# One DiT layer in float32 on one core: mod rounds written out, square sums on VectorE, three full low-rank tiles, 512-column matmuls in merge, output and down

## What is computed

```
mod   = silu(c) @ w_mod + b_mod                    # 6 x 2048 values, also for the context
h     = rmsnorm(x) * (1 + sc1) + sh1               # and the same for the context tokens
p     = h @ w_in                                   # k, r, v, 4 x 96 low-rank, 256 gate columns, u, v, gates
y     = rwkv7(dwconv1d(p...))                      # both directions, over context and latents
yg    = gelu(u) * (w_spatial @ LN(gelu(v)) + b)    # chunk MLP
m     = sigmoid(ga) * (y @ w_proj_a) + sigmoid(gb) * (yg @ w_proj_b)
x     = x + gt1 * rmsnorm(m @ w_out)
h2    = rmsnorm(x) * (1 + sc2) + sh2
x     = x + gt2 * rmsnorm((silu(a) * b) @ w_down)  # a, b = dwconv2d(h2 @ w_up)
```

## Time and profile before

| | us |
|---|---|
| median of 3 runs | 2997.85 (2994.82 to 2999.31) |
| the profiled execution | 2995.07 |
| its span, first to last instruction | 2993.1 |
| PE busy in it | 2841.4 (95%) |
| DVE busy | 1839.5 (61%) |
| ACT busy | 1002.5 (33%) |
| stages by the timeline: mod to 115.5, lora to 192.3, pairs to about 1656, gv and gu to 1741.5, merge to 2071.3, out to 2174, up to 2711, down to 2975 | |

### The profile page before, as it was taken

One profiled execution on the slowest core, in us unless ns is written; L12 is line 12 of the kernel. 1 busy time (PEld: TensorE's weight loads), 2 busy tenths in 40 slices (PEclk: granted clock), 3 DMA queues, 4 the chain that ended last, 5 costly groups with the idle time before them and its releaser, 6 DMA issues.

```text
span 2993.1 us, 70020 instructions
## 1 busy us (share of the span) xinstructions
PE 2841.4 (95%) x27808; PEld 2207.5 (74%) x27808; DVE 1839.5 (61%) x3324; ACT 1002.5 (33%) x1715; POOL 579.6 (19%) x708
## 2 busy tenths in 40 slices
PE   5899999999999999999989999999989999999997
PEld 1246665566656566666556699999979999999997
DVE  1115666677666767666675544444378888885434
ACT  1123322333322333332231433333354444443333
POOL 0003222333122233222231110000013333330000
PEclk9799999999999999999999999999989999999998
DMA  8621332222332222233214545554525555554553
GB/s 323 268 77 63 107 107 93 70 74 89 103 107 93 82 75 86 93 106 107 79 53 148 204 148 182 186 182 170 198 99 183 182 182 182 182 182 156 182 174 134
DMA packets 75291, 412.28 MB, mean 138 GB/s; under 512 B 9200, under 2 KB 11888, under 8 KB 42736
## 3 DMA queue, kind: packets, MB, share of 16 engines
q1 hardware_dynamic: 74352, 407.51, 39.5%
q0 software_dynamic: 768, 2.10, 0.2%
HBM read 405.38 MB, written 4.19 MB: 137 GB/s over the span
## 4 chain that ended last, share of the span: by engine, by line
PE 84%; DVE 8%; issue 3%; DMA 3%; ACT 1%; SPq 0%; DVEq 0%; ACTq 0%; PEldq 0%
PE PB L671 18%; PE Q L919 6%; PE Q L920 6%; PE Q L924 6%; PE PB L919 4%; PE PB L920 4%; PE PB L924 4%; PE CH L924 3%; PE CH L920 3%; PE CH L919 3%; DMA ring<-w_mod_dram 3%; PE Q L808 3%; PE PB L656 2%; PE Q L794 2%; PE Q L815 2%
## 5 line engine op out<-in xcount | busy, mean ns | idle before, releaser
L671 PE MATMUL PB<-hT,ring 128*128 128x512 f32 (+1 forms) x1536 | 673.5, 552 | 6.4 <-PEq L660 5.4
L1615 DVE TENSOR_TENSOR w_lo_r<-ring,w_hi_r 128x1536 fp32r<-128x1536 f32 (+3 forms) x178 | 386.9, 2174 | 269.8 <-ACT w_hi_r L1217 269.8
L1217 ACT ACTIVATE w_hi_r<-ring 128x2048 fp32r<-128x2048 f32 (+2 forms) x178 | 325.8, 1831 | 453.7 <-PE Q L924 211.3
L671 PEld LDWEIGHTS PB<-hT,ring 128*128 128x128 f32 x1536 | 256.8, 189 | 120.9 <-issue 70.7
L920 PE MATMUL PB<-hT_r,w_hi_r 128*128 128x256 f32 x832 | 204.6, 285 | 0.0
L1475 DVE SCALAR_TENSOR_TENSOR arena<-ring,csilp,arena 128x512 f32<-128x512 f32 x240 | 193.5, 806 | 5.2 <-DMA ring<-w_mod_dram 1.0
L1775 DVE TENSOR_TENSOR w_lo_r<-ring,w_hi_r 128x1408 fp32r<-128x1408 f32 x62 | 101.2, 1633 | 147.9 <-ACT w_hi_r L1331 147.9
L1876 POOL TENSOR_TENSOR w_lo_r<-ring,w_hi_r 128x512 fp32r<-128x512 f32 x88 | 118.4, 1346 | 361.4 <-ACT w_hi_r L1217 361.4
L919 PE MATMUL PB<-hT_r,w_hi_r 128*128 128x256 f32 x704 | 175.7, 289 | 4.7 <-DVE hT_r L1702 4.7
L919 PE MATMUL Q<-ff_hi_r,w_hi_r 128*128 128x256 f32 x704 | 175.6, 288 | 1.8 <-ACT w_hi_r L1331 1.8
L920 PE MATMUL Q<-ff_lo_r,w_hi_r 128*128 128x256 f32 x704 | 172.9, 284 | 0.0
(11 more groups left out here) (266 smaller groups left out, 6096.5 us busy)
## 6 DMA issues: line engine op xcount, KB each, us to landing
ring<-w_up_dram SPq DMA_DIRECT2D x88, 1024.0 KB, 4.8
ring<-w_mod_dram SPq DMA_DIRECT2D x128, 512.0 KB, 3.7
ring<-w_rkv_dram SPq DMA_DIRECT2D x48, 1024.0 KB, 5.8
ring<-w_down_dram SPq DMA_DIRECT2D x64, 704.0 KB, 4.0
ring<-w_mod_dram SPq DMA_DIRECT2D x32, 1024.0 KB, 7.8
ring<-w_ga_dram SPq DMA_DIRECT2D x16, 1024.0 KB, 4.8
ring<-w_gb_dram SPq DMA_DIRECT2D x16, 1024.0 KB, 4.8
ring<-w_pa_dram SPq DMA_DIRECT2D x16, 1024.0 KB, 4.8
```

The costliest lines, as they stand in the source:

```text
L671: last = mm(PB[slot % 2][:, 0:cols], tile(n, kt), hT[:, kt, 0:cols], start=(kt == 0), stop=(kt == KT - 1))
L1217: f(w_hi_r[:, r % 2, 0:n], ring[:, r, 0:n], ACT.Copy).then_inc(hi_rdy, 1)
L1615: tt(w_lo_r[:, r, 0:n], ring[:, r, 0:n], as_f32(w_hi_r[:, r % 2, 0:n]), ALU.subtract).then_inc(lo_rdy, 1)
```

## The change

- **Constants and x.** Six constants (those that mod needs) are loaded first; the other eight follow behind the first lora weight tile, on a semaphore of their own (`consts2_ld`), for which ACT, DVE, PE (before the first `item`) and POOL wait. x comes in four quarters behind the four regions of mod round 0.
- **Mod rounds.** The loop is written out. The rounds alternate between banks Q[0] and Q[1]; the sums of round i-1 stand between the second and third region of round i, the last ones inside the first lora tile (before kt 4).
- **Square sums.** ACT squares by quarters; DVE adds the 16 tiles down to one; PE runs one 512-column matmul against ones in round 2. `hT` is scaled by quarters in rounds 3 to 6, and a quarter of h is made (DVE and ACT) as soon as its column gains are there, in rounds 4 to 7.
- **Low-rank columns.** The 384 columns are packed in 3 tiles of 128; five DMAs inside SBUF move the rows to the four places of 96 that the heads read. `lora` loads go from (2, 2, 1, 1) to (2, 1, 1, 1): the last gate tile is in region 0. The heads' first projection waits for bank 0 only; sigmoid and moves are waited for before the first `item`.
- **512 columns.** In merge, out and down the two 256-column matmuls with w_hi become one with 512 columns (hi and lo side by side), w_lo goes on into one half, and DVE adds the two halves of the bank (`halves`, a tensor_reduce). ACT takes sigmoid and square from SBUF after that. For the gates the high half of h is copied next to the low one by ACT in gu round 1. gu and up keep 256 columns.
- **Tables.** Three `preload_act_table_set` for the set with Ln and Exp are added: before the gv statistics, before out, and before down (one at the start was there).

```diff
-            for t, name in ((ident, "ident"), (ones, "ones"), ... 13 constants
+            for t, name in ((part_sum, "part_sum"), (scal, "scal"), (ones, "ones"), (bmod, "bmod"), (gains, "gains")):
                 sp.dma_start(t[:], io[name]).then_inc(consts_ld, 16)
-            sp.dma_start(hT[:], io["xT_all"]).then_inc(x_ld, 16)
-            with sp.Fori(0, 8) as i:
+            for i in range(8):
                 for r in range(4):
+                    load(r, "mod", 0, i, 1, io["w_mod"][i * 4 + r])
+                if i == 0:
+                    for g in range(4):
+                        sp.dma_start(hT[:, 4 * g:4 * g + 4], io["xT_all"][:, 4 * g:4 * g + 4]).then_inc(x_ld[g], 16)
...
+            for i in range(8):
+                mod_tiles(i, 0, 2)
+                if i:
+                    sums(i - 1)
+                mod_tiles(i, 2, 4)
+                if i == 2:
+                    pe.wait_ge(sq_rdy, 5)
+                    mm(Q[3][:, :], ones[:, :], x_sq[:, 0], start=True, stop=True).then_inc(ssq_ps, 1)
...
-            for n in range(6):
+            for n in range(5):
                 r = n % 4
                 region(r, "lora", n // 4, 0, 0)
                 if n >= 2:
                     pe.wait_ge(lo_cv, n - 1)
                 for kt in range(KT):
                     if n == 0:
+                        if kt == 4:
+                            sums(7)
...
-            pe.wait_ge(lo_cv, 6)
-            pe.wait_ge(lo_act, 4)
+            pe.wait_ge(lo_cv, 4)
             pe.sem_inc(pb_free[0], 1)
-            pe.sem_inc(pb_free[1], 1)
...
+            sp.wait_ge(lo_act, 2)
+            sp.wait_ge(lo_cv, 3)
+            for to, dst, n, src in ((1, 0, 0, slice(LORA, P)), ...
+                sp.dma_start(lora_act[dst:dst + src.stop - src.start, to], packed[n][src]).then_inc(lora_mv, 16)
...
+            def high_pair(bank, r, k, both, start):
+                mm(bank[:, :], w_hi_r[:, r % 2, k * P:(k + 1) * P], both, start=start, stop=False)
...
                     for kt in range(n):
-                        with_high(Q[r][:, 0:T], r, kt, hi[:, kt], lo[:, kt], kt == 0)
+                        high_pair(Q[r], r, kt, both[kt], kt == 0)
...
+            def halves(out, bank):
+                return nc.vector.tensor_reduce(out, bank[:, :].rearrange("p (a b) -> p b a", a=2), mybir.AxisListType.X, ALU.add)
...
             def out_four(i):
                 for r in range(4):
                     highs("out", i, r, 4, "up")
-                    product(r, "out", 0, i, 1)
-                    f(mixT..., four[r][:, 0:T], ACT.Copy)
-                    f(sq..., four[r][:, 0:T], ACT.Square).then_inc(o_sb, 1)
+                    act.wait_ge(o_sum, i * 4 + r + 5)
+                    f(sq..., mixT..., ACT.Square).then_inc(o_sb, 1)
...
             with dve.Fori(0, 3) as i:
                 for r in range(4):
                     low("out", i, r + 2)
+                    out_sum(i, r)
...
-                product(3, "down", q, i, 2)
-                f(mixT..., Q[2 + q][:, 0:T], ACT.Copy)
-                f(sqd[q], Q[2 + q][:, 0:T], ACT.Square).then_inc(dn_sb, 1)
+                act.wait_ge(dn_sum, i * 2 + q + 3)
+                f(sqd[q], mixT..., ACT.Square).then_inc(dn_sb, 1)
+            act.preload_act_table_set("natural_log_exp_and_others")
```

More of the change, by code:

```diff
@@ L46 @@
 NPARX = 24
-PHASES = [("mod", (8, 8, 8, 8)), ("lora", (2, 2, 1, 1)), ("pair", (PAIRS, PAIRS, PAIRS, 0)),
+PHASES = [("mod", (8, 8, 8, 8)), ("lora", (2, 1, 1, 1)), ("pair", (PAIRS, PAIRS, PAIRS, 0)),
           ("gv", (2, 2, 2, 2)), ("gu", (2, 2, 2, 2)), ("merge", (KT,) * 4), ("out", (4,) * 4),
@@ L244, in layer_kernel @@
         consts_ld = sem("consts_loaded")
-        x_ld = sem("x_loaded")
+        consts2_ld = sem("pair_consts_loaded")
+        lora_mv = sem("lora_rows_moved")
+        x_ld = [sem(f"x_quarter{g}_loaded") for g in range(4)]
         seen = sem("waits_seen")
@@ L612, in mod_sums @@
                 last.then_inc(mod_sum, 1)
[L614 to L619, removed]
             pe.wait_ge(consts_ld, 16 * NCONST)
@@ L1082, in _ @@
+            squares(0)
+            squares(1)
             mod_copy(0)
+            squares(2)
+            squares(3)
             mod_copy(1)
-            rms(1, rstd[:, :], Q[1][:, :], TT)
-            with act.Fori(2, 8) as i:
+            mod_copy(2)
+            rms(1, rstd[:, :], Q[3][:, :], TT)
+            for i in range(3, 6):
                 mod_copy(i)
-            act.wait_ge(gcol_rdy, 1)
-            for kt in range(KT):
-                f(hT[:, kt, T:TT], hT[:, kt, T:TT], ACT.Identity, scale=gcol[:, kt, 1:2],
-                  bias=modT[:, kt, 1:2]).then_inc(hc_rdy, 1)
@@ L1098, in _ @@
+            act.wait_ge(lo_cv, 5)
             for n in range(2):
-                f(lora_act[0:LORA, n], lora_act[0:LORA, n], ACT.Tanh).then_inc(lo_act, 1)
-            for n in range(4, 6):
-                f(gate_act[:, n - 4], gate_act[:, n - 4], ACT.Sigmoid).then_inc(lo_act, 1)
+                f(gate_act[:, n], gate_act[:, n], ACT.Sigmoid).then_inc(lo_act, 1)
             act.wait_ge(par_rdy, 1)
@@ L1673, in _, with out_sum @@
             merge_four(KT - 1)
+            def out_sum(i, r):
+                product(r, "out", 0, i, 1)
+                halves(mixT[:, bass.ds(i * 4 + r, 1), :].rearrange("p a b -> p (a b)"), four[r]).then_inc(o_sum, 1)
             with dve.Fori(0, 3) as i:
@@ L1934, in host_layout @@
     t["w_rkv"] = rkv.reshape(3 * PAIRS, P, REG)
[L1935 removed]
+    t["w_lora"] = tiles(w[:, off:o_g])
     t["w_gate"] = tiles(w[:, o_g:o_u])
```

208 lines of the change are left out of this document (134 added, 74 removed).

## The result

| | before | after |
|---|---|---|
| median of the runs | 2998.44 us (4 runs, 2994.82 to 2999.31) | 2947.62 us (4 runs, 2945.57 to 2949.74) |
| profiled execution: time, span | 2995.07, 2993.1 | 2949.74, 2947.8 |

The ratio is 0.9833, with a 95% interval of 0.9816 to 0.9850: 50.8 us less, where 75.3 were forecast. 2947.6 lies above the range (2908 to 2942). Of the two profiled executions the one before is among the quickest of its kernel and the one after the slowest, so the traces lie only 45.3 us apart.

The account below looks back on a forecast made before the run. PE's matmuls were taken to bound the later stages and `w_mod`'s DMA the start; savings of 29.7 (start-up), 44.9 (512-column pairs) and 0.7 us (hand-overs) sum to 75.3, taking the median 2997.85 to 2922 us, range 2908 to 2942.

Parts of the forecast that it names:

- The stream of `w_mod`: Mod rounds: PE's square sums stop the weight DMA for 11.2 us; the change should remove that stop.
- DVE's adds: Square sums of x in the mod rounds: adding tiles on DVE takes 6 us in all, hidden before PE asks.
- The first tile, three tiles for four: Low-rank stage: the first lora tile ends 15.5 us earlier, and one tile less saves 13.7 us.
- the last sums: Eight small matmuls, now inside the first lora tile: cost between nothing and 1.93 us, taken as 1.5.
- The low clock in this tile: First lora tile: PE comes out of half-idle rounds, so the extra 2.7 us over other tiles is kept.
- The gap before the heads: Before the heads' first projection: PE's wait of 5.4 becomes 4.9 us, on the weight DMA into region 0; 0.5 saved.
- 512 columns: Merge, out, down: each of 1856 matmul pairs goes from 240 to 215.8 ns, 44.9 us saved (39 to 50).
- Rival 1: Merge, out, down: columns, not weight loads, cost 120 ns, so 512-column matmuls save nothing; 2967 us, chance 6%.
- The half clock: At clock 0.50 a 256-column matmul takes only its columns, 213 to 215 ns; read as evidence against rival 1's stream limit.
- Halves: Merge, out, down: DVE's sum of bank halves takes 0.69 us; out's chain of 5.5 us just fits its 5.8 us tile.
- Hand-overs: Between stages: +1.6 into out, +2.7 at its last square, +0.4 ending down, -5.4 from tables; sum -0.7 us.
- the price of 2.7 us a switch: The Trainium skill's table-load cost at three norms: would save 14 us, total 84; the prediction kept 1.28 and 5.4.

## Why the prediction was wrong, point by point

- **The stream of `w_mod`**: right, in size and cause. The squares put back on PE bring 11.1 us of stop back, 11.2 were read. The region itself came at 97.5, 1.5 later than forecast, as the MiB took 2.53 us and not 2.48. One term inside was wrong and cost nothing: DVE's adds, put at 6 us, took 8.8 (2.29, 4.61, 1.22 and 0.69), still ahead of PE.
- **The first tile, three tiles for four**: right. The first tile ends 16.9 us earlier (15.5 forecast), the tiles are 13.7 us each. That the start came out 1.3 us better than forecast, in spite of the late region, is in part luck: the last sums took 0.95, not 1.5, and the clock was full from the tile's start. The low clock in this tile, on which the prediction kept 2.7 us, does come in other kernels' traces: without the three tables the tile takes 17.8 us instead of 15.0, its first 5 us at clock 0.50.
- **The gap before the heads**: right, 5.05 for 4.9, and the reason (region 0) holds: with another region the wait is gone.
- **512 columns: the step that failed.** The prediction put "So a pair goes from 240 to 215.8, 24.2 ns saved", from a float32 row, with 39 us as its lower bound. A pair goes to 228 in merge, 12 ns saved, some 22 us in all. The direction was right: joining two matmuls saves one fixed cost. Which one was not: it is 13.3 ns that each fp32r matmul pays at full clock, and the joined one pays it too, so a pair saves it once, and not twice less 2.5. The row of float32 was the wrong neighbour; its type pays 2.5 ns and not 13.3. Rival 1, nothing saved, was as far off on the other side; the bound that was missing lay between them, "one of the two 13 ns stays": 240 - 13.3 = 226.7. Why fp32r pays it is open.
- **The half clock** was the hint that was read too far. There the 13 ns are not seen. That speaks against a limit per column, as the prediction said, but not against a fixed cost that stays with each matmul.
- **Halves**: right, 0.68 us for 0.69. In output DVE's low part, sum and ACT's square end 5.6 us after the tile (5.5 forecast), and PE doesn't wait.
- **Hand-overs**: the forecast ones came as told (+1.4 for +1.6 into output, +2.3 for +2.7 at its last square, 5.1 for 5.4 from the tables, where the price of 2.7 us a switch that the prediction named beside it would have given 14). One was left out: the preload for the last norm was costed at nothing, as ACT is idle for most of down, but it stands in ACT's queue just ahead of a high part that PE waits for. 1.4 us of wait and 1 us of low clock behind it, 2.4.
- **The rest**: 22.6 and 2.4 are 25.0, where 24.5 are missing between the medians and 30.0 between the two traces. The 5 us more of the traces are mostly the heads and pair stage, untouched, which gave 3.4 back, and the chunk MLP with 1.3. But in the thirteen traces of this case the heads and pair stage is between 1458.9 and 1467.2 us long, and two traces of the changed kernel lie 3.7 apart. That is scatter; its cause is open. So the 25.0 agree with the 24.5 no better than some us.

## What to carry over

A fixed cost per instruction is only hidden by making it longer if it runs beside the instruction; if it is added to each, joining two saves it once. So before a price is taken from a neighbouring type, take two column counts of the same type and separate slope and constant; and where only one count is in the trace, let the bounds include "one of two stays". Read the step inside a block of equal matmuls, not across its ends. A table load has no free place in an idle engine's queue as such: look at what stands behind it and who waits.

## What the runs showed of the chip

- At full granted clock an fp32r matmul with 128 weight columns costs its columns at 2.4 GHz and 13.3 ns (256, 384, 512 columns); a bfloat16 matmul and a float32 record cost 2.5. What the 13.3 ns are is open: the bank, the form of the operand and the rows make no difference, the number of weight columns makes one.
- fp32r weights of 128 columns are followed by the next no faster than every 111.7 ns (128 and 192 columns), those of 64 columns every 60. So an fp32r matmul with 128 weight columns gains nothing from fewer than some 236 columns, an estimate from (111.7 - 13.3) x 2.4.
- 64 weight columns made a 512-column fp32r matmul no faster but 3.3 ns slower (230.0 for 226.7), a 256-column one 3 ns faster (116.7 for 119.9). Not explained. 64 rows changed nothing.
- After a PE wait of 6.8 us the next 16 matmuls took 5.7 us, at a mean granted clock of 0.63; with idle matmuls in the wait they took 3.75 at 1.00.
